# Handing the tokens over in turned layout, with the norm weights moved into the projection weights and the root mean square into the evacuations

## The reference, cut to what matters

```
def _rmsnorm(x, g):
    xf = x.astype(jnp.float32)
    y = xf * lax.rsqrt(jnp.mean(xf * xf, axis=-1, keepdims=True) + EPS)
    return (y * g.astype(jnp.float32)).astype(x.dtype)
...
qa, ka, va, za, qr, fr, ir, zr = _project(_rmsnorm(hp, norm_g[l]), w_in[l])   # u = xn @ w, eight slices
...
hp = hp + _merge(oa, orec, za, zr, subln_g[l], rec_norm_g[l], lam_init, w_out[l])
```

## Time and profile before

| | |
|---|---|
| median of 3 runs | 1574.97 us (1574.3 to 1575.33) |
| the profiled execution: time, span | 1575.97 us, 1574.3 us |
| mean granted TensorE clock | 0.984 |
| PE busy | 1509.5 us, 96% of the span |
| DVE, ACT, POOL busy | 928.2, 859.2, 680.6 us |

### The profile page before, as it was taken

How to read it: one execution, slowest core, us unless ns; L and a number is a source line. 1 busy time by engine, 2 the same in 40 slices (tenths; PEclk the granted TensorE clock), 3 DMA queues, 4 the chain that set the end, 5 groups by cost and what they waited for, 6 DMA issues and landing times.

```text
span 1574.3 us, 25558 instructions
## 1 busy us (share of the span) xinstructions
PE 1509.5 (96%) x8432; PEld 1293.2 (82%) x8432; DVE 928.2 (59%) x2087; ACT 859.2 (55%) x2325; POOL 680.6 (43%) x1407
## 2 busy tenths in 40 slices
PE   5999999998999999989999999899999999699997
PEld 4888888887888888868888888688888888588886
DVE  6676666676555566675555667665556657433232
ACT  5666666665555655565565555755565566321121
POOL 6655555535644433446454433655544433300000
PEclk9999999998999999999999999999999999799999
DMA  7242221153422222134322221314222110433431
GB/s 229 85 144 95 95 94 68 71 159 108 131 97 68 68 67 68 46 110 126 104 71 68 68 68 65 116 56 150 69 91 74 54 51 17 153 120 133 147 120 67
DMA packets 99431, 149.11 MB, mean 95 GB/s; under 512 B 10288, under 2 KB 79792, under 8 KB 90608
## 3 DMA queue, kind: packets, MB, share of 16 engines
q1 hardware_dynamic: 99312, 147.62, 28.7%
HBM read 103.03 MB, written 44.56 MB: 94 GB/s over the span
## 4 chain that ended last, share of the span: by engine, by line
PE 85%; DVE 5%; issue 3%; ACT 2%; POOL 2%; SPq 1%; DMA 1%; POOLq 0%; DVEq 0%; ACTq 0%
PE pab L570 42%; PE oar L640 7%; PE qkb L691 7%; PE pab L731 6%; PE qkb L731 6%; PE qkb L596 6%; PE tb L631 3%; DVE scores L1112 2%; PE tb L670 2%; PE tb L718 1%; SPq L305 1%; PE oar L612 1%; PE oar L609 1%; PE oar L611 1%; PE tb L536 1%
## 5 line engine op out<-in xcount | busy, mean ns | idle before, releaser
L570 PE MATMUL pab<-w_hi,xr 128*128 128x512 f32 x2176 | 785.6, 404 | 2.6 <-issue 2.4
L570 PEld LDWEIGHTS pab<-w_hi,xr 128*128 128x128 f32 x2176 | 413.9, 190 | 83.2 <-issue 3.6
L570 PE MATMUL pab<-w_lo,xr 128*128 128x512 f32 x1088 | 428.4, 394 | 0.0
L1316 POOL TENSOR_TENSOR dd<-dd 128x64 f32<-128x64 f32 x340 | 118.0, 347 | 459.3 <-DVE dd L1097 459.3
L570 PEld LDWEIGHTS pab<-w_lo,xr 128*128 128x128 f32 x1088 | 207.8, 191 | 33.2
L691 PE MATMUL qkb<-kp,q 128*128 128x512 f32 (+3 forms) x656 | 186.9, 367 | 21.6 <-DVE kp L1060 19.8
L828 ACT ACTIVATE fb<-pab 128x256 f32<-128x256 f32 x68 | 26.1, 385 | 274.4 <-PE pab L570 274.4
L1112 DVE CUSTOM_DVE_ANT_0 scores<-qkb,bias 128x512 f32<-128x512 f32 (+4 forms) x136 | 84.9, 625 | 153.1 <-PE qkb L691 153.1
L883 ACT ACTIVATE scores<-scores,nmx 128x128 f32<-128x128 f32 (+16 forms) x136 | 156.9, 1164 | 16.4 <-DVE nmx L1122 16.4
L691 PEld LDWEIGHTS qkb<-kp,q 128*128 128x128 f32 x656 | 120.6, 190 | 53.6 <-DVE kp L1060 21.2
L640 PE MATMUL oar<-vv,at 128*128 128x128 f32 x1104 | 152.5, 277 | 1.9 <-ACT at L849 1.9
(11 more groups left out here) (143 smaller groups left out, 2625.1 us busy)
## 6 DMA issues: line engine op xcount, KB each, us to landing
xr<-xs SPq DMA_DIRECT2D x51, 1024.0 KB, 5.3
xs<-xr SPq DMA_DIRECT2D x17, 1024.0 KB, 3.9
w_raw<-in_w_in SPq DMA_DIRECT2D x48, 256.0 KB, 5.8
mix<-mx SPq DMA_DIRECT2D x68, 128.0 KB, 2.2
bias<-mix SPq DMA_DIRECT2D x17, 512.0 KB, 5.0
w_raw<-in_x_prompt SPq DMA_DIRECT2D x16, 512.0 KB, 3.9
scores<-in_x_prompt SPq DMA_DIRECT2D x16, 512.0 KB, 4.2
out<-vv SPq DMA_DIRECT2D x16, 512.0 KB, 3.0
```

The lines of the kernel that those rows point to most:

```text
L570: last = mm(pab[:, b, :], x, w[:, kt, 512 * b:512 * b + 512], start=(kt == 0 and part == 0 and w is w_hi), stop=(kt == KT - 1 and part == 1))
L1316: g.tensor_tensor(o[:, :, 0, :], ref, c[:, :, 0, :], sub)
```

## The change

The host now hands over two further arrays: x_turned, each tile of the tokens already turned (model dimension on the partitions), and norm_turned, norm_g as a 128 x 8 array. In the kernel:

- The eight transposes for each tile (x_transposes), their waits on PE, and x_normalise on DVE are gone. SP loads a tile twice, turned (turned_load) and as rows (rows_load), the rows only for the sum of squares.
- x_high and x_low read the turned tile from SBUF, not tb in PSUM; x stays unnormalised.
- norm_g goes into the weights of the four heads: as the scale of ACT's w_hi copies (a 128 x 1 operand), as the scalar of DVE's w_lo instruction (now SCALAR_TENSOR_TENSOR), and on POOL as an instruction of its own, which scales the raw piece in place before the subtraction, with a wait between them. w_out's pieces are as before.
- POOL's row_scale becomes x_scale for the tiles of x: three instructions instead of two, with 1 / rms and -1 / rms kept for every tile (xrs, nrs). Ten of the evacuations that ACT makes of pab for a tile now take one of these as scale, a 128 x 1 operand instead of none or a constant; DVE's nb becomes a SCALAR_TENSOR_TENSOR.
- The order at the start: w_in's b = 1 half is loaded before the rows of tile 0, tile 1 after all of w_in.
- In a head's last tile split_qk now stands ahead of DVE's b = 0 pieces.

```
@@ sync
+            def turned_load(t):
+                if t > 1:
+                    sp.wait_ge(S["x_lo"], t - 1)
+                sp.dma_start(x_raw[t % 2], x_turned[t]).then_inc(S[f"xt_in{t % 2}"], 16)
             def rows_load(t):
                 if t > 1:
-                    sp.wait_ge(S["x_rows"], t - 1)
+                    sp.wait_ge(S["x_sq"], t - 1)
...
+            sp.dma_start(gn[:, :], norm_turned[:, :]).then_inc(S["gains_in"], 16)
+            turned_load(0)
+            for kt in range(KT):
+                raw_load(0, 1, kt)
             rows_load(0)
-            sp.dma_start(x_gain, norm_g[0:1, :].to_broadcast([P, D_MODEL])).then_inc(S["gains_in"], 16)
-            for kt in range(2):
-                raw_load(0, 1, kt)
-            rows_load(1)
-            for kt in range(2, KT):
-                raw_load(0, 1, kt)
             for kt in range(KT):
                 raw_load(0, 0, kt)
+            turned_load(1)
+            rows_load(1)
...
                             rows_load(t + 2)
+                            turned_load(t + 2)
@@ tensor
-            def x_transposes(t):
-                pe.wait_ge(S["x_rows"], t + 1)
-                if t >= 2:
-                    need(pe, 0, "t_evac", t_use["qk", t - 2] + 1)
-                if t > 0:
-                    pe.wait_ge(S["x_lo"], t)
-                for kt in range(KT):
-                    last = tr(tb[:, kt // 4, P * (kt % 4):P * (kt % 4) + P], x_norm[:, P * kt:P * kt + P],
-                              ident[:, :])
-                last.then_inc(S["x_t"], 1)
...
-                        if first and kt == (2 if t > 0 else KT - 1) and t < NT - 1:
-                            x_transposes(t + 1)
...
-                if first and t + 2 < NT:
-                    pe.wait_ge(S["x_lo"], t + 3)
...
-                if first and t + 1 < NT:
-                    pe.wait_ge(S["x_lo"], t + 2)
@@ scalar
-                F(xr[:, t % XRING, 0], tb[:, :, :], ACT.Copy).then_inc(S["x_hi"], 1)
+                F(xr[:, t % XRING, 0].rearrange("p k c -> p (k c)"), x_raw[t % 2], ACT.Copy).then_inc(S["x_hi"], 1)
...
-                    F(w_hi[:, kt, 512 * b:512 * b + 512], raw_piece(h + 1, b, kt), ACT.Copy
+                    gain = gn[:, kt:kt + 1] if h + 1 < HEADS else 1.0
+                    F(w_hi[:, kt, 512 * b:512 * b + 512], raw_piece(h + 1, b, kt), ACT.Copy, scale=gain
...
+                scale = xrs[:, t:t + 1]
...
-                F(vv[:, slot_of(t), :], pa[:, 2 * P:3 * P], ACT.Copy)
+                F(vv[:, slot_of(t), :], pa[:, 2 * P:3 * P], ACT.Copy, scale=scale)
...
-                F(ez[:, 0, :], pa[:, 3 * P:4 * P], ACT.Exp, scale=-1.0).then_inc(S["a_evac"], 1)
+                F(ez[:, 0, :], pa[:, 3 * P:4 * P], ACT.Exp, scale=nrs[:, t:t + 1]).then_inc(S["a_evac"], 1)
@@ vector
-            def x_normalise(t):
-                dve.wait_ge(S["x_rs"], t + 1)
-                stt(x_norm, x_raw[t % 2], trs[:, 0:1], x_gain, ALU.mult, ALU.mult).then_inc(S["x_rows"], 1)
...
-                tt(nb[:, :], pab[:, 1, 0:P], rc[:, 0, :], ALU.mult).then_inc(S["pb_free"], 1)
+                stt(nb[:, :], pab[:, 1, 0:P], xrs[:, t:t + 1], rc[:, 0, :], ALU.mult, ALU.mult).then_inc(S["pb_free"], 1)
...
                         split_weights(h, 1, (4, 5, 7))
-                        if h < HEADS - 1:
-                            split_weights(h, 0, (0, 1, 3))
                     split_qk(h, t)
+                    if t == SAMPLE and h < HEADS - 1:
+                        split_weights(h, 0, (0, 1, 3))
@@ gpsimd
+            def x_scale(t):
+                pool.wait_ge(S["x_sq"], t + 1)
+                setup_link(g.tensor_scalar(xms[:, t:t + 1], xsq[:, t:t + 1], 1.0 / D_MODEL, EPS, ALU.mult, ALU.add))
+                setup_link(g.tensor_tensor(xrs[:, t:t + 1], xms[:, t:t + 1], half[:, 0:1], ALU.pow))
+                g.tensor_scalar(nrs[:, t:t + 1], xrs[:, t:t + 1], -1.0, None, ALU.mult).then_inc(S["x_rs"], 1)
...
+                    out, raw, high = w_lo[:, kt, half_], raw_piece(h + 1, b, kt), w_hi[:, kt, half_].bitcast(f32)
+                    if h + 1 < HEADS:
+                        g.tensor_scalar(raw, raw, gn[:, kt:kt + 1], None, ALU.mult).then_inc(S["w_scaled"], 1)
+                        need(pool, h + 1, "w_scaled", lo_of(b, kt)[1])
+                    g.tensor_tensor(out, raw, high, ALU.subtract).then_inc(S["w_lo_pool"], 1)
```

More of the change, by code:

```diff
@@ L193, in build @@
         rs = sb("rs", [P, 2])
+        gn = sb("gn", [P, KT])
+        xsq = sb("xsq", [P, NT])
+        xms = sb("xms", [P, NT])
+        xrs = sb("xrs", [P, NT])
+        nrs = sb("nrs", [P, NT])
         tsq = sb("tsq", [P, 2])
@@ L793, in _ @@
             F(lbw[:, 2:4, :], lbw[:, 0:2, :], ACT.Exp).then_inc(S["setup_exp"], 1)
-            x_high(1)
             def copy_decayed_keys(h, t):
@@ L825, in recurrence_columns @@
             def recurrence_columns(h, t):
                 need(act, h, "proj_b", t + 1)
+                if h == 0:
+                    act.wait_ge(S["x_rs"], t + 1)
                 pb = pab[:, 1, :]
-                F(fb[:, 0:2, :].rearrange("p g c -> p (g c)"), pb[:, 0:2 * P], ACT.Exp, scale=-1.0)
-                link(h, F(fb[:, 2, :], pb[:, P:2 * P], ACT.Exp))
+                scale, minus = xrs[:, t:t + 1], nrs[:, t:t + 1]
+                F(fb[:, 0:2, :].rearrange("p g c -> p (g c)"), pb[:, 0:2 * P], ACT.Exp, scale=minus)
@@ L837, in gate_sigmoids @@
+                F(ez[:, 1, :], pb[:, 3 * P:4 * P], ACT.Exp, scale=minus).then_inc(S["b_evac"], 1)
             def gate_sigmoids(h, t):
@@ L990, in split_weights @@
                     half_ = slice(512 * b, 512 * b + 512)
-                    tt(w_lo[:, kt, half_], raw_piece(h + 1, b, kt), w_hi[:, kt, half_].bitcast(f32), ALU.subtract
-                       ).then_inc(S["w_lo_vec"], 1)
+                    out, raw, high = w_lo[:, kt, half_], raw_piece(h + 1, b, kt), w_hi[:, kt, half_].bitcast(f32)
+                    if h + 1 < HEADS:
+                        low = stt(out, raw, gn[:, kt:kt + 1], high, ALU.mult, ALU.subtract)
+                    else:
+                        low = tt(out, raw, high, ALU.subtract)
+                    low.then_inc(S["w_lo_vec"], 1)
             v.memset(ones[:, :], 1.0)
             dve.wait_ge(S["gains_in"], 16)
-            x_normalise(0)
-            split_weights(-1, 1, (0,))
             x_low(0)
-            split_weights(-1, 1, (1, 3))
-            x_normalise(1)
-            split_weights(-1, 1, (4, 5, 7))
+            split_weights(-1, 1, (0, 1, 3, 4, 5, 7))
             split_weights(-1, 0, (0, 1, 3, 4, 5, 7))
+            x_low(1)
             dve.wait_ge(S["const_in"], 80)
@@ L1152, in head @@
                         combine(*before, h)
-                    if first and t == 0:
-                        x_low(1)
                     if t == SAMPLE:
@@ L1159, in head @@
                         split_weights(h, 1, (3,))
-                    if first and t + 2 < NT:
-                        x_normalise(t + 2)
                     if first and t == 0:
@@ L1248, in split_weights @@
                     half_ = slice(512 * b, 512 * b + 512)
-                    g.tensor_tensor(w_lo[:, kt, half_], raw_piece(h + 1, b, kt), w_hi[:, kt, half_].bitcast(f32),
-                                    ALU.subtract).then_inc(S["w_lo_pool"], 1)
-            row_scale("x_sq", "x_rs", 1, 0)
-            split_weights(-1, 1, (2,))
-            row_scale("x_sq", "x_rs", 2, 0)
-            split_weights(-1, 1, (6,))
+                    out, raw, high = w_lo[:, kt, half_], raw_piece(h + 1, b, kt), w_hi[:, kt, half_].bitcast(f32)
+                    if h + 1 < HEADS:
+                        g.tensor_scalar(raw, raw, gn[:, kt:kt + 1], None, ALU.mult).then_inc(S["w_scaled"], 1)
+                        need(pool, h + 1, "w_scaled", lo_of(b, kt)[1])
+                    g.tensor_tensor(out, raw, high, ALU.subtract).then_inc(S["w_lo_pool"], 1)
+            split_weights(-1, 1, LO_POOL)
+            x_scale(0)
             split_weights(-1, 0, LO_POOL)
+            x_scale(1)
             name, n = lo_of(0, 3)
@@ L1329, in head @@
                     if first and t + 2 < NT:
-                        row_scale("x_sq", "x_rs", t + 3, 0)
+                        x_scale(t + 2)
                     if t == SAMPLE:
@@ L1366 @@
     arrays, args = {}, []
+    turned = np.zeros((NT, P, KT, P), np.float32)
+    turned[:PT] = np.asarray(inputs["x_prompt"])[0].reshape(PT, P, KT, P).transpose(0, 3, 2, 1)
+    turned[PT, :, :, :DEC] = np.asarray(inputs["x_sample"])[0].reshape(DEC, KT, P).transpose(2, 1, 0)
+    laid = dict(inputs, x_turned=turned.reshape(NT, P, KT * P),
+                norm_turned=np.asarray(inputs["norm_g"])[0].reshape(KT, P).T)
     for name in _INS:
-        a = np.ascontiguousarray(inputs[name])
+        a = np.ascontiguousarray(laid[name])
         arrays[f"in_{name}"] = a
```

56 lines of the change are left out of this document (28 added, 28 removed).

## The result

The changed kernel takes 1565.41 us (median of 4 runs, 1564.65 to 1567.62), the kernel before 1575.15 in the same comparison: ratio 0.9941, 95% interval 0.9924 to 0.9959. It is faster by 9.7 us. The forecast was 1561.3 with a range of 1549 to 1570; the time is in the range, 4.1 us above the forecast.

A forecast was written before the change was run, and what follows sets the result against it. PE's own work, 85% of the chain, was taken as the bound. Savings of 12.8, 1.7 and 2.4 less a loss of 3.2 gave 13.7 us off the profiled 1575.97, hence a median of 1561.3 us, range 1549 to 1570.

The forecast's parts named there:

- the transposes of head 0: Head 0, tiles 2 to 16: PE's transposes and their waits go, saving 12.8 us.
- ACT's operands: All heads: evacuations with a 128x1 scale take 0.10 us longer each; four heads lose 3.2 us, 0.8 each.
- The start and tile 1: Start and tile 1 of head 0: gates turn 0.85 us earlier, 0.9 less for transposes; 1.7 us saved.
- I let these cancel: Start: POOL's late exponents of tile 0 against DVE having no x_normalise ahead of the bias table; net nothing.
- its own terms, 1.0 and twice 1.0: ACT's operands: 1.0 us through existing waits for qn and at, twice that for steps now just in time.
- rival in which they reach the path in every tile: Every tile: ACT's longer evacuations delay PE; at 0.4 us a tile 27 us are lost, 1585 us; chance 5%.
- The borders: After heads 0, 1 and 2: kp's wait goes, kq's comes; 0.8 us saved each, 2.4 us in all.
- the low clock: Borders: PE idles again and its clock falls to 0.50, costing 2.2 us behind rec_scores.
- rival that POOL's scaling pays the borders back: Borders: two POOL instructions where one stood, each up to 3.27 us; 8.4 us more, 1569.7 us; chance 13%.
- rival of open borders: Borders: only split_qk was late and kq is in time; 24 us more saved, 1537, half of it 1549; chance 14%.
- The last part: Last border (w_out) and epilogue: no scaling, order kept, only some 0.3 us added; left out of the sum.

The follow-up runs named there:

- half_turned: Kernel before, with PE transposing only four of the eight blocks of x from tile 1 on; 1567.73 us, ratio 0.9957.
- kp_late: Changed kernel with split_qk put back behind DVE's three pieces of b = 0; 1572.42 us, ratio 0.9983 to the kernel before.
- decay_first: Changed kernel with DVE's kq of the sample tile ahead of its three b = 0 pieces in heads 0 to 2; 1569.71 us.
- before_kp: Kernel before, with only split_qk of the sample tile moved ahead of DVE's three b = 0 pieces in heads 0 to 2; 1571.66 us, ratio 0.9983.
- before_ops: Kernel before, with ACT's ten evacuations of every tile taking their scale from a column of 1.0 or -1.0; 1577.08 us, ratio 1.0015.
- masks_first: Changed kernel with POOL's w_lo pieces given to DVE, plus POOL's seventeen masks ahead of x_scale(0); 1553.17 us, ratio 0.9865 to the kernel before.
- no_scale: Changed kernel without POOL's scaling instruction, so two of eight low pieces lack the gain; 1562.01 us, ratio 0.9921 to the kernel before.
- start_pool: Changed kernel with x_scale(1) and x_scale(2) moved behind POOL's gates of tile 0; 1566.20 us, ratio 0.9943 to the kernel before.
- kq_between: Changed kernel with POOL's w_lo pieces given to DVE, plus kq between DVE's second and third b = 0 piece in heads 0 to 2; 1558.48 us.

## Why the prediction was right, and where it was not

**Faster, by the transposes of head 0: right.** The term was -12.8; the profile has -11.7 for the same tiles, and half_turned shows that most of it is PE's own work. The -11.7 also holds what ACT's operands cost in head 0, some 0.5 us if it is as in heads 1 and 2. Tile 3 gave 1.39, so some of its DMA wait went too.

**The start and tile 1: the step that failed.** The prediction gave -1.7, from a gate turn 0.85 earlier and 0.9 of transposes, and said of POOL's late exponents and DVE's missing x_normalise: "I let these cancel". The gate turn was better than that, -1.4. But POOL came 5.1 us later to the exponents (39.09 against 34.01); 4.0 of them came back, because the subtractions no longer met DVE's bias table, and 1.1 stayed. So kq came 1.1 later, PE waited 2.45 us for it, and neither the earlier gate turn nor the transposes of tile 1 came through: tile 1 grew by 2.4, and the term was +1.0 instead of -1.7. The low clock was not the cause in this profile: it had ended at 39.3, and PE still had to wait for kq at 47.13. Other profiles spread: tile 1 took 21.2, 22.8 and 24.4 us in three kernels with the same start (the changed one, kp_late, decay_first) against 18.8, 20.0 and 19.5 in three with nearly the start of before (before, before_kp, before_ops), so a mean over them would make the term about +2. Most of the spread of the first three lies behind rec_scores, which started at 47.1, 47.4 and 47.6: kp_late ran 3.4 us at half clock from 48.6 and decay_first 6.8 us from 46.7. masks_first shows the cause: with POOL's masks out of the way tile 1 loses 4.8 us, and its 17.69 are 1.1 below the kernel before, near the prediction's 0.9. What was left out was to follow POOL's queue through the start; before the change it already idled 5.84 us ahead of its first piece (12.05).

**ACT's operands: right in mechanism and size.** +3.2 was set (its own terms, 1.0 and twice 1.0, add up to 3.0). Heads 1 to 3 grew by 0.5, 0.5 and 1.2, and 0.5 of the last is a wait for POOL's w_lo in its first tile, not ACT; in no_scale all three grew by 0.5. before_ops measured 2.7 for all four heads. The rival in which they reach the path in every tile is out: 63 us of ACT's time cost 2 to 3.

**The borders: right in what replaces what; the parts were mis-sized.** kp's wait went, kq's came, the low clock followed. At the border of heads 1 and 2 rec_scores started 21.8 us behind the gate turn of tile 16 instead of 26.1: 4.3 earlier, where the prediction had 3.0. Behind it 4.2 us were lost and not 2.2: to the low clock, and to a second wait that the sum did not have, for POOL's piece of b = 0 (1.38 here, 0.96 at the others). The gain was 1.1 us for three borders in the profile of the changed kernel and 3.5 in that of start_pool, which has the same borders; the 2.4 of the prediction lies between, and that it does is partly luck. POOL's scaling took 1.56 to 2.53 us (1.5 was set). The rival that POOL's scaling pays the borders back did not come: they lost nothing, and leaving the scaling out gives 3.4 us, where the rival had 8.4. The rival of open borders is out; in kq_between the next products of DVE's queue took the gain.

**The last part** was left out of the sum and gave -1.4 in the profiles. The longer stretch of half clock in it was 10.2 us instead of 13.7. But the same part takes 241.39 us in before_kp, with the end of before (242.57 there), and 242.18 in kp_late, with that of the changed kernel (241.16 there), so little of the 1.4 can be called a gain.

**The sum.** -13.7 was set; the profiles gave -10.9, the medians -9.7. The start is off by 2.7, the borders by 1.3, head 0 by 1.1, ACT by -0.9, and the uncounted end by -1.4. Only the first is clear of the spread between profiles.
